# Two-block decoder on one core: the order of the beginning is changed (first weight slot in two pieces, x fetched after six slots, a table fetch moved back)

## The reference

```
mk, mv = jnp.split(mem @ w_kv, 2, axis=-1)      # w_kv = mem_w_kv[l], [1024, 512]
```

```
y = x32 * lax.rsqrt(jnp.mean(x32 * x32, axis=-1, keepdims=True) + EPS)    # rmsnorm of x
proj = (y * g) @ a_w_in[0]
```

## Time and profile before

| | us |
|---|---|
| median of 3 runs | 1604.61 (1603.79 to 1605.31) |
| the profiled execution | 1605.0 |
| its span | 1603.2 |
| PE busy in the span | 1585.8 (99%) |
| DVE busy | 1091.2 (68%) |
| ACT busy | 919.7 (57%) |

### The profile page before, as it was taken

The page is one execution under the profiler, slowest core; times in us unless marked ns, Lnnn a source line. Parts: engine busy times, 40 slices in busy tenths (PEclk is TensorE's granted clock), DMA queues, the critical chain, the costliest instruction groups (busy, mean ns, idle before and its releaser), DMA issues.

```text
span 1603.2 us, 23557 instructions
## 1 busy us (share of the span) xinstructions
PE 1585.8 (99%) x9239; PEld 1353.9 (84%) x9239; DVE 1091.2 (68%) x1759; ACT 919.7 (57%) x1553; POOL 56.7 (4%) x98
## 2 busy tenths in 40 slices
PE   7999999999999999999999999999999999999998
PEld 6888888889888888888887788888888889888887
DVE  5877776778676767665677466567666667775665
ACT  5756755567665546644476564457454474664544
POOL 4010000000030000000002100000000000000000
PEclk9999999999999999999999999999999999999999
DMA  8555666555356655666655465664665664456662
GB/s 284 161 157 169 221 225 193 185 161 167 117 178 200 190 186 181 198 186 189 190 161 170 125 203 176 199 192 159 214 191 186 185 196 148 119 177 202 186 187 76
DMA packets 212402, 288.20 MB, mean 180 GB/s; under 512 B 11097, under 2 KB 180383, under 8 KB 212293
## 3 DMA queue, kind: packets, MB, share of 16 engines
q1 hardware_dynamic: 208500, 280.00, 55.5%
q0 software_dynamic: 3792, 6.70, 1.6%
HBM read 284.99 MB, written 3.88 MB: 180 GB/s over the span
## 4 chain that ended last, share of the span: by engine, by line
PE 94%; DVE 2%; DMA 1%; ACT 1%; issue 0%; SPq 0%; POOL 0%; DVEq 0%
PE two L2199 88%; PE two L2276 1%; PE two L2445 1%; DVE w_lo L1471 1%; PE two L2458 1%; DMA x_tok<-in_x 1%; PE two L2468 1%; DVE qk L1827 1%; PE two L2828 0%; PE two L2262 0%; DMA vals<-u_dram 0%; ACT w_hi L852 0%; PE two L2471 0%; DMA u_dram<-aux 0%; DVE misc L1805 0%
## 5 line engine op out<-in xcount | busy, mean ns | idle before, releaser
L2199 PE MATMUL two<-act_parts,w_hi 128*128 128x512 f32 (+1 forms) x2784 | 801.7, 353 | 0.0
L1471 DVE TENSOR_TENSOR w_lo<-raw,w_hi 128x1024 fp32r<-128x1024 f32 (+1 forms) x520 | 613.1, 1220 | 114.7 <-ACT w_hi L852 114.2
L2199 PE MATMUL two<-act_parts,w_lo 128*128 128x256 f32 x2256 | 635.0, 281 | 0.0
L2199 PEld LDWEIGHTS two<-act_parts,w_hi 128*128 128x128 f32 x2784 | 487.0, 188 | 81.1 <-issue 5.3
L852 ACT CAST w_hi<-raw 128x1024 fp32r<-128x1024 f32 (+1 forms) x520 | 516.4, 1049 | 6.5 <-DMA raw<-in_ffn_w_up 4.6
L2199 PEld LDWEIGHTS two<-act_parts,w_lo 128*128 128x128 f32 x2256 | 425.5, 189 | 2.1
L2199 PE MATMUL two<-w_hi,act_parts 128*128 128x512 f32 (+2 forms) x832 | 248.8, 379 | 2.9 <-ACT w_hi L852 2.8
L981 ACT COPY p_sb<-two 128x512 f32<-128x512 f32 x108 | 62.4, 578 | 247.1 <-PE two L2199 247.1
L2199 PE MATMUL two<-w_hi,hid_even 128*128 128x512 f32 x576 | 187.8, 393 | 0.0
L2199 PEld LDWEIGHTS two<-w_hi,act_parts 128*128 128x128 f32 x832 | 151.0, 189 | 33.7 <-ACT w_hi L852 3.2
L1599 DVE TENSOR_TENSOR pt_sb<-two,p_sb 128x512 f32<-128x512 f32 x54 | 37.3, 691 | 198.5 <-ACT p_sb L981 198.5
(11 more groups left out here) (317 smaller groups left out, 1193.5 us busy)
## 6 DMA issues: line engine op xcount, KB each, us to landing
raw<-in_ffn_w_up SPq DMA_DIRECT2D x160, 512.0 KB, 4.0
raw<-in_ffn_w_down SPq DMA_DIRECT2D x132, 512.0 KB, 3.5
raw<-in_ffn_w_gate SPq DMA_DIRECT2D x80, 512.0 KB, 3.8
raw<-in_a_w_in SPq DMA_DIRECT2D x24, 512.0 KB, 4.7
raw<-in_fox_w_in SPq DMA_DIRECT2D x20, 512.0 KB, 3.8
raw<-in_ffn_w_up SPq DMA_DIRECT2D x32, 256.0 KB, 3.6
raw<-in_w_kv SPq DMA_DIRECT2D x12, 512.0 KB, 3.7
raw<-in_mem_w_kv SPq DMA_DIRECT2D x8, 512.0 KB, 11.1
```

The source lines that it names most:

```text
L1471: nc.vector.tensor_tensor(w_lo[:, r, 0:n], raw[:, r, 0:n], w_hi[:, r, 0:n], ALU.subtract).then_inc(lo_done, 1)
L2199: return nc.tensor.matmul(dst, a, w, start=start, stop=stop, skip_group_check=True)
```

## The change

The left half of the first memory block is fetched first, then slot 0 in two DMAs of 256 KB (one row chunk each; the first with the new semaphore `first_in`), then the right half of the memory block. ACT rounds slot 0 in two casts of 512 columns (`half_hi`; the first counts the new semaphore `hi_half`, the second `hi_done`). PE does block (0, 0) between the transposes of the left and of the right half, and block (0, 1) ahead of the transposes of the second memory block; the first two matmuls of a block with slot 0 wait for `hi_half` alone. SP issues slots 4 and 5 ahead of the two blocks of x. ACT fetches the exponential table after slots 4 and 5 and not before them. DVE does the first `take_mem` between the subtractions of slots 4 and 5.

```diff
@@ sync @@
-            for half in range(2):
+            def mem_half(half):
                 sp.dma_start(mem_tok[:, 0, half * HALF:(half + 1) * HALF],
                              mem[0, 0:P, half * HALF:(half + 1) * HALF]).then_inc(mem_in[half], 16)
-            group("M0", mem_w_kv[0], 0, [0, 1])
+
+            def half_slot(k):
+                sp.dma_start(raw[:, 0, k * HALF:(k + 1) * HALF],
+                             mem_w_kv[0][k * P:(k + 1) * P, 0:HALF]).then_inc(landed[0] if k else first_in, 16)
+
+            mem_half(0)
+            half_slot(0)
+            half_slot(1)
+            mem_half(1)
+            group("M0", mem_w_kv[0], 0, [1])
             sp.dma_start(mem_tok[:, 1, :], mem[0, P:2 * P, :]).then_inc(mem_in[2], 16)
             group("M0", mem_w_kv[0], 0, [2, 3])
+            group("M1", mem_w_kv[1], 0, [0, 1])
             for b in range(NTB):
                 sp.dma_start(x_tok[:, b, :], x[0, b * P:(b + 1) * P, :]).then_inc(x_in[b], 16)
-            group("M1", mem_w_kv[1], 0)
+            group("M1", mem_w_kv[1], 0, [2, 3])
@@ scalar @@
+            def half_hi(k):
+
+                act.wait_ge(landed[0] if k else first_in, 16)
+                nc.scalar.copy(w_hi[:, 0, k * HALF:(k + 1) * HALF],
+                               raw[:, 0, k * HALF:(k + 1) * HALF]).then_inc(hi_done if k else hi_half, 1)
+
             mem_hi(0, 0)
-            splits(0)
+            half_hi(0)
+            half_hi(1)
+            split[0] = 1
             mem_hi(0, 1)
             splits(1)
...
             for b in range(NTB):
                 moment_x(0, b)
+            splits(5)
             fetch_table(ACT.Exp)
-            splits(5)
             turned("M0", mk[:, 0, :, 0:P], 0, 2)
@@ vector @@
                 root_x(0, b)
+            splits(4)
+            take_mem(0, 0)
             splits(5)
-            take_mem(0, 0)
             take_mem(0, 1)
@@ tensor, first_slot @@
-                pe.wait_ge(hi_done, a + i + 1)
                 pe.wait_ge(al, 8 * b + (4 if i < 2 else 8))
                 for k in range(per):
                     c = per * i + k
+                    if i == 0 and k == 0:
+                        pe.wait_ge(hi_half, 1)
+                    else:
+                        pe.wait_ge(hi_done, a + i + 1)
                     mm(pj[b], act_part(0, c, b), hi[:, k, :], c == 0, False)
                     mm(pj[b], act_part(1, c, b), hi[:, k, :], False, False)
@@ tensor @@
             turn_mem(0, 0)
+            first_slot(0, 0)
             turn_mem(0, 1)
-            first_slot(0, 0)
+            first_slot(0, 1)
             turn_mem(1, 0)
             turn_mem(1, 1)
-            first_slot(0, 1)
```

More of the change, by code:

```diff
@@ L432, in build @@
         va_rounded = sem("va_rounded")
+        first_in = sem("first_in")
+        hi_half = sem("hi_half")
         hi_done = sem("hi_done")
```

## The result

The changed kernel takes 1606.67 us in the median of 20 runs (1605.62 to 1609.23), the kernel before 1604.78 (1603.79 to 1606.02). The ratio is 1.0014, 95% interval 1.0008 to 1.0021: 1.9 us slower, which is within the 0.2% that were called no change, and shown by that many runs all the same. The forecast was 1605.5 (1603.5 to 1607.8). The profiled execution took 1606.48 with a span of 1604.7 us, against 1605.0 and 1603.2.

What follows compares the result with a forecast made beforehand. PE, busy 99% of the span, was taken as the bound, so only its idle time counts. Slot 6 read 0.9 us later, added to the median 1604.61, gave 1605.5 us, range 1603.5 to 1607.8.

Steps and rivals of the forecast that it cites:

- x lands at 18.9: Opening: x's first block, sent behind slots 4 and 5, lands at 18.9 us instead of 16.16, 2.74 us later.
- DVE comes to slot 6 at 27.5: Opening: DVE begins slot 4 at 23.0, needs 4.49 us for six pieces of work, and reaches slot 6 at 27.5.
- PE's own chain: Opening: 2.1 us won at block (0, 0), paid back twice over in two gaps; parameters done at 25.8 or 24.4.
- rival B: Slot 0's second piece lands only with the right half, at 7.36; PE's chain moves 1.5 us, 1606.8 us; chance 0.12.
- either is at or before DVE's 28.75, so the chain of x decides, or ties: At slot 6: PE asks at about 28.7 or 27.8, no later than DVE is ready, so x's landing sets the time.
- +0.9: At slot 6: PE reads it at 28.75 instead of 27.84, and this delay is carried to the end.
- The clock: PE's opening: TensorE's clock rises late or early; parameters at 25.8 or 24.4, slot 6 wanted at 28.7 or 27.8.
- Table fetch and copy order: Ahead of slot 6: no table fetch before the casts saves 1.41 us; the copy precedes slot 5's subtraction, keys ready at 24.9.
- x's chain: From x's landing to slot 6: 9.85 us instead of 11.68, 1.83 less, against x landing 2.74 later, leaving +0.91.
- Rival A: Opening: x lands sooner, at 17.6, clock up by block (0, 1); slot 6 0.4 us earlier, 1604.2 us; chance 0.16.

Runs made afterwards that it cites:

- e1: The change with x fetched ahead of slots 4 to 7 again, all else as in the change; 1606.72 us, ratio 1.0013 to the kernel before.
- e4: The kernel before with the table fetched after the casts of slots 4 and 5 and the first memory-value copy between their subtractions; 1603.44 us, ratio 0.9992.
- e5: The change with 8, 6, 10 and 8 transposes of the identity, results unread, added in PE's idle time; 1605.12 us, ratio 1.0002 to the kernel before.
- e9: e4 with added identity transposes, 8 ahead of the memory's and 10 behind those of its first block; 1602.46 us, ratio 0.9986 to the kernel before.
- e10: The change with x first, block (0, 1) after the second memory block's transposes, and 8, 6 and 8 added identity transposes; 1602.07 us, ratio 0.9984.
- e7: e4 with added identity transposes, 8 ahead of the memory's and 20 behind those of its first block; 1602.37 us, ratio 0.9984 to the kernel before.
- e6: The change with e1's early x and e5's added transposes together; 1603.06 us, ratio 0.9992 to the kernel before.
- e3: The head: only the change's early part (slot 0 in pieces, PE's order), x, table and copies as in the kernel before; 1607.14 us, ratio 1.0015.
- e11: The changed kernel itself, unaltered, run again for a second profile; 1606.24 us.
- e12: The changed kernel itself, unaltered, run again for a third profile; 1607.30 us.

## Why the prediction was right in sign and short in size

- **x lands at 18.9.** It landed at 18.58, right within 0.3. (It stood behind 3.0 MB and stands behind 4.0 MB, not 2.5 and 3.5 as the section on the change has it; the exchange of places and the 1.0 MB between them, on which the forecast rests, are right.)
- **DVE comes to slot 6 at 27.5.** It did at 27.55, by two errors that cancel: it began slot 4 at 22.44 and not at 23.0, since x came 0.3 sooner and the moments took 2.75 us and not 3.02, and it lost 0.54 us at 24.21 waiting for PE.
- **PE's own chain.** Block (0, 0) at 6.3, block (0, 1) at 11.7, gaps of 1.7 and 0.8 to 1.1: measured 6.27, 11.81, 1.77 and 1.09. The parameters were to be done at 25.8 with a late clock and were, at 25.96. ACT had cast both pieces by 6.45 (5.31 + 1.14), ahead of the 7.36 of rival B, which falls.
- **The step that failed: "either is at or before DVE's 28.75, so the chain of x decides, or ties".** In the profile PE's chain decided: by 0.18 us against DVE as it came, and DVE itself had stood 0.54 us behind PE. In e1's profile, with x early, PE decides as well. Two links were overlooked. ACT casts slot 6 behind its copy of the turned keys, so slot 6 follows the keys by 3.05 us (25.96 to 29.01), not by an earliest 2.8. The prediction let ACT be through with that cast at about 26.7; the copy waited 1.50 us for PE, and DVE could begin only at 27.73. And DVE's first `take_mem` waits for PE's last block of b = 0.
- **The size.** +0.9 was forecast; the opening of the profile shows +1.2, the wait at 890 us another 0.25, the medians +1.9. The clock was the term with too narrow a range: I let it rise early or late, once, and took the two to differ by nothing that counts. Before, PE's 1.6 us of idle time hid a rise at 12.65. The change used that idle time up, so that now all of it reaches the end: keys at 24.55 (e1), 25.96 and 27.51 for the same order on PE (0.64 of the last for a late landing). This also fits the wider scatter, 3.6 us among 20 runs against 2.2, though no run without a profile shows its clock.
- **Table fetch and copy order.** Costed inside the sum of x's chain; by themselves they win 1.2 us (e4), which the new order on PE spends. Head +2.5 and e4's -1.2 leave +1.3, and the change measured +1.9; the difference is within the intervals.
- **Rival A** (x sooner than 18.0, clock up early) did not come about in the change: x landed at 18.58 and the clock was late. In e1's profiled execution both held, and the keys came 0.18 us ahead of before (24.55, not 24.73); in the median e1 gained nothing.

## What to carry to other kernels

An early first product can be worth nothing by itself: follow that engine to the next point where it joins another, and count each wait that the new order puts between. Idle time ahead of such a join hides a clock that rises late; a change that uses it up also buys the scatter of the clock. And where two chains meet within a few tenths of a microsecond, an experiment on one of them can show nothing until the other is shortened too, as with x here, so run the single edits and the pair.

## What the runs showed of the hardware that was not expected

- **Transposes raised the clock in three of five kernels.** In e5 PE did 18 transposes and nothing else from 2.00 us, and the first product after them ran at the full level (four matmuls in 1.20 us). So it was in e9 and e10. It is not so each time: in e7, with 8 + 8 + 20 of them, the last 20 took 4.47 us, 0.22 each against 0.125 for the ten at 9.06 in e5 (1.25 us), and the clock rose only within the first product; in e6, with the same 18 as in e5, the first product's four took 1.84 us. The Trainium skill, "TensorE: Matmul & The Clock Gate", section "Part 4: PE-mode transpose", says that transposes in TensorE's transpose mode do not count as busy time for the full clock as matmuls do. For these float32 transposes of 128x128 the traces of e5, e9 and e10 show otherwise; they list them as MATMUL, so whether they are of the kind that the page means stays open.
- **The clock's rise isn't fixed by the program.** With the same instructions on PE up to 13 us, block (0, 1) ran at the low level in the profiles of the change, of e3 and of e11 and at the full one in those of e1 and e12, and in e12 the clock went down again behind the gap.
- **Late waits vary by themselves.** The wait for `vals<-u_dram` at about 890 us was 1.31 us before, 1.54 in the change, 0.75 in e12, 0.20 in e5, and 0 in e7; the change's own three profiles have 1.54, 1.28 and 0.75. A single profile's end is thus uncertain by over a microsecond, and an edit of the beginning is better read from the keys and from slot 6 than from the span.
